# Feed-forward gate and value products with tokens on partitions instead of features, and PE transposes behind them

## The reference

```python
# block 1: a depthwise causal convolution over 3 tokens stands between the products and the gelu
h = rms_norm(x, norm_ffn_w[i])
u = causal_depthwise_conv(h @ w_ffn_up[i], w_ffn_conv[i], b_ffn_conv[i])
u_gate, u_val = jnp.split(u, 2, axis=-1)
x = x + (jax.nn.gelu(u_gate) * u_val) @ w_ffn_down[i]
# block 2
h2 = rms_norm_2(x, g_ffn[i])
x = x + (jax.nn.silu(h2 @ w_gate[i]) * (h2 @ w_up[i])) @ w_down[i]
```

## Time and profile before

| | |
|---|---|
| median of 3 runs | 2569.82 us (2569.43 to 2570.0) |
| span of the profiled execution, first to last instruction | 2567.5 us |
| median less span | 2.3 us |
| PE busy | 2548.9 us, 99% |
| DVE busy | 1534.1 us, 60% |
| ACT busy | 1082.9 us, 42% |
| mean granted TensorE clock | 0.997 |

### The profile page before, as it was taken

One profiled execution on the slowest core, in us unless ns is written; L12 is line 12 of the kernel. 1 busy time (PEld: TensorE's weight loads), 2 busy tenths in 40 slices (PEclk: granted clock), 3 DMA queues, 4 the chain that ended last, 5 costly groups with the idle time before them and its releaser, 6 DMA issues.

```text
span 2567.5 us, 37759 instructions
## 1 busy us (share of the span) xinstructions
PE 2548.9 (99%) x16088; PEld 2305.2 (90%) x16088; DVE 1534.1 (60%) x1280; ACT 1082.9 (42%) x967; POOL 41.7 (2%) x57
## 2 busy tenths in 40 slices
PE   8999999999999999999999999999999999999998
PEld 8988778999999999998888888889999999999987
DVE  4556555666666666676677656555555555555564
ACT  4344444444434444446544433343333333333353
POOL 0000000000000000000000000000000000000000
PEclk9999999999999999999999999999999999999999
DMA  7555465555555555555665555655555555555553
GB/s 263 180 155 169 147 229 185 181 180 185 191 180 188 187 180 190 185 181 184 214 201 168 181 190 186 226 180 182 190 184 181 191 184 183 192 181 186 189 188 110
DMA packets 237966, 476.77 MB, mean 186 GB/s; under 512 B 9958, under 2 KB 10534, under 8 KB 237110
## 3 DMA queue, kind: packets, MB, share of 16 engines
q1 hardware_dynamic: 234102, 459.72, 54.5%
q0 software_dynamic: 3744, 15.77, 1.8%
q10 hardware_dynamic: 32, 0.01, 0.0%
HBM read 471.28 MB, written 4.19 MB: 185 GB/s over the span
## 4 chain that ended last, share of the span: by engine, by line
PE 98%; issue 1%; DMA 0%; DVE 0%; ACT 0%; SPq 0%; POOLq 0%; POOL 0%; ACTq 0%
PE acc L1402 49%; PE acc L1395 45%; PE aux L1425 1%; DMA raw<-in_w_in 0%; PE aux L1488 0%; PE aux L1469 0%; PE aux L1567 0%; PE aux L1461 0%; PE aux L1460 0%; PE aux L1527 0%; PE aux L1552 0%; PE aux L1557 0%; ACT w_hi L595 0%; PE aux L1578 0%; PE aux L1489 0%
## 5 line engine op out<-in xcount | busy, mean ns | idle before, releaser
L1395 PE MATMUL acc<-act_hi,w_hi 128*128 128x256 f32 x3216 | 912.9, 284 | 2.5 <-DVE w_lo L822 2.5
L1395 PE MATMUL acc<-act_lo,w_hi 128*128 128x256 f32 x3216 | 911.0, 283 | 0.0
L1395 PE MATMUL acc<-act_hi,w_lo 128*128 128x256 f32 x3216 | 910.9, 283 | 0.0
L1402 PE MATMUL acc<-w_hi,act_hi 128*128 128x512 f32 x1888 | 740.8, 392 | 0.0
L1402 PE MATMUL acc<-w_hi,act_lo 128*128 128x512 f32 x1888 | 735.1, 389 | 0.0
L1402 PE MATMUL acc<-w_lo,act_hi 128*128 128x512 f32 x1888 | 735.1, 389 | 0.0
L601 ACT ACTIVATE w_hi<-raw 128x2048 fp32r<-128x2048 f32 x216 | 413.9, 1916 | 738.0 <-PE acc L1395 501.7
L822 DVE TENSOR_TENSOR w_lo<-raw,w_hi 128x2048 fp32r<-128x2048 f32 (+2 forms) x225 | 504.5, 2244 | 355.4 <-ACT w_hi L595 355.4
L595 ACT ACTIVATE w_hi<-raw 128x2048 fp32r<-128x2048 f32 (+2 forms) x225 | 422.5, 1879 | 673.3 <-PE acc L1402 490.0
L827 DVE TENSOR_TENSOR w_lo<-raw,w_hi 128x2048 fp32r<-128x2048 f32 x216 | 495.2, 2293 | 343.6 <-ACT w_hi L601 343.5
L1395 PEld LDWEIGHTS acc<-act_hi,w_hi 128*128 128x128 f32 x3216 | 616.7, 192 | 6.9 <-issue 5.7
(11 more groups left out here) (146 smaller groups left out, 737.5 us busy)
## 6 DMA issues: line engine op xcount, KB each, us to landing
raw<-in_w_in SPq DMA_DIRECT2D x104, 1024.0 KB, 5.2
raw<-in_w_ffn_up SPq DMA_DIRECT2D x88, 1024.0 KB, 5.0
raw<-in_w_ffn_down SPq DMA_DIRECT2D x44, 1024.0 KB, 5.1
raw<-in_w_gate SPq DMA_DIRECT2D x44, 1024.0 KB, 5.2
raw<-in_w_up SPq DMA_DIRECT2D x44, 1024.0 KB, 5.2
raw<-in_w_down SPq DMA_DIRECT2D x44, 1024.0 KB, 5.0
raw<-in_w_ple_gate SPq DMA_DIRECT2D x32, 1024.0 KB, 5.1
raw<-in_w_out SPq DMA_DIRECT2D x16, 1024.0 KB, 5.0
```

The source lines that it names most:

```text
L1395: mm = pe.matmul(flat[0:rows, T * f:T * f + T], w[:, c], x[:, k, :], start=start and n == 0 and f % 2 == 0, stop=stop and n == 2, skip_gro ...
L1402: mm = pe.matmul(acc[:, s, m, 0:width], x[:, k, c], w, start=start and n == 0, stop=stop and n == 2, skip_group_check=True)
```

## The change

All gate and value units use the unflipped form. Their results have tokens on partitions, so the norm factor is the per-partition scalar `r_col`, and `norm_diag` and `norm_row` are dropped for both feed-forward stages. In block 1, ACT evacuates (`up_out`) in two operations into `up_tok`; PE transposes (`up_turn`, 8 transposes) into a half of `aux`, once for the gate and once for the value of every step (22 times), and the convolution reads `aux` instead of `up_in`. In block 2, ACT evacuates the gate with the silu (`gate_silu`), DVE multiplies the value accumulator into it (`up_product`), and PE transposes the finished product (`f_turn`, once a step, 11 times); ACT and DVE split it from `aux` (`f_split`, `f_rest`). The small work moves to other slots.

```diff
+            def up_out(part, g, slot, used):          # ACT
+                act.wait_ge(unit_used, used)
+                act.wait_ge(acc_free, g)
+                act.wait_ge(r_done, 2)
+                own.order()
+                step(ACT.Copy, up_tok[part][:, 0, :], acc[:, (slot + FFN[0]["g"]) % 2, 0, :], scale=r_col[:, 0:1])
+                act.activation(up_tok[part][:, 1, :], acc[...], ACT.Copy, scale=r_col[:, 1:2]).then_inc(acc_free, 1)
+            def conv_first(it, part):                 # ACT, instead of ffn_a
+                act.wait_ge(up_turned, it * 2 + (part + 1))
+                act.wait_ge(tables_now, it + 1)
+                own.order()
+                for f in range(KU):
+                    step(ACT.Identity, (f_gate, f_val)[part][:, f, :], fours((aux01, aux23)[part])[:, f, :], conv_a,
+                         scale=conv_now[:, TAPS - 1, part, f:f + 1], bias=conv_now[:, TAPS, part, f:f + 1])
...
 # ACT, block 1: head
-                head = {3: lambda: ffn_a(b, 0, 0, g0 + 1), 5: lambda: ffn_act(b, 0, g0 + 1),
-                        7: lambda: ffn_a(b, 0, 1, g0 + 2)}
+                head = {3: lambda: up_out(0, g0, 0, u0 + 4), 4: lambda: conv_first(0, 0)}
...
+                gelu(0)
+                up_out(1, g0 + 1, 1, u0 + 8)
 # ACT, block 1: each round, after the split of slot j
+                        if j == 0:
+                            conv_first(i, 1)
+                        if j == 2:
+                            f_split(0, i)
+                        if j == 3:
+                            up_out(0, i * 6 + (g0 + 2), 0, i * 12 + (u0 + 12))
+                        if j == 4:
+                            conv_first(i + 1, 0)
...
 # DVE, block 1: each round, before the remainder of slot j
                         if j == 1:
-                            ffn_c(b, i)
+                            conv_rest(i, 1)
+                            f_product(i)
                         if j == 2:
-                            ffn_d(b, i)
+                            conv_tables(i + 1)
                         if j == 3:
-                            ffn_a(b, i + 1, 0, g0 + 2, i * 12 + (u0 + 12))
+                            f_rest(0, i)
...
 # DVE, block 1: tail
+                tail = {2: lambda: conv_tables(last), 3: lambda: f_rest(0, last - 1),
+                        5: lambda: conv_rest(last, 0), 11: lambda: f_rest(0, last, KU)}
                 for j in range(12):
...
                     if j >= 8:
-                        add_down(gt + j - 6, j - 8, ut + j + 1)
+                        add_down(gt + j - 6, gt + j - 6, j - 8, ut + j + 1)
+                    if j == 9:
+                        conv_rest(last, 1)
+                        f_product(last)
                     remainder(ut + j + SPL)
...
 # PE
+                def up_turn(step, p, g):
+                    pe.wait_ge(acc_free, g + 1)
+                    if p or not isinstance(step, int) or step:
+                        pe.wait_ge(conv_b, step * 8 + (4 if p else -4))
+                    for k in range(KU):
+                        for m in range(M):
+                            c = T * k + P * m
+                            mm = pe.transpose((aux01, aux23)[p][:, c:c + P], up_tok[p][:, m, P * k:P * k + P], ident[:])
+                    mm.then_inc(up_turned, 1)
...
-                        mm = part(f["act"], KU * q, u, g, True, q == 0, q == 3)
+                        mm = part(f["act"], KU * q, u, g, False, q == 0, q == 3)
...
 # PE, each round, after unit n
+                        if n == 0 and b == 0:
+                            up_turn(i, 1, i * 6 + (g0 + 1))
+                        if n == 4 and b == 0:
+                            up_turn(i + 1, 0, i * 6 + (g0 + 2))
+                        if n == 0 and b == 1:
+                            f_turn(i, i * 6 + (g0 + 1))
...
 # PE, head (block 1): up_turn after unit 4; tail: up_turn after units 0, 4 and 8 (block 1), f_turn after 0 and 8 (block 2)
```

More of the change, by code:

```diff
@@ L78, in __init__, with did @@
         self.eng, self.n, self.last, self.i, self.per = eng, {}, None, None, {}
-    def did(self, sem):
+    def did(self, sem, at=None):
+        if at is not None:
+            self.last = (sem, at)
+            return
         base = self.n[sem.num] = self.n.get(sem.num, 0) + 1
@@ new lines, in conv_first, with gelu @@
+            def conv_first(it, part):
[5 more added lines that the diff above has]
+                         scale=conv_now[:, TAPS - 1, part, f:f + 1], bias=conv_now[:, TAPS, part, f:f + 1])
+            def gelu(it):
+                act.wait_ge(conv_b, it * 8 + 4)
+                own.order()
+                step(ACT.Gelu_apprx_tanh, f_gate, f_gate, act_f)
@@ new lines, in gate_silu, with f_split @@
+            def gate_silu(g, slot, used):
+                act.wait_ge(unit_used, used)
+                act.wait_ge(acc_free, g)
+                act.wait_ge(r_done, 5)
+                own.order()
+                step(ACT.Silu, gate_tok[:, 0, :], acc[:, (slot + FFN[1]["g"]) % 2, 0, :], scale=r_col[:, 0:1])
+                act.activation(gate_tok[:, 1, :], acc[:, (slot + FFN[1]["g"]) % 2, 1, :], ACT.Silu, scale=r_col[:, 1:2]).then_inc(acc_free, 1)
+            def f_split(b, it, tile=0):
+                f = FFN[b]
+                if b == 0:
+                    act.wait_ge(f_full, it + 1)
@@ L707, in ffn_act @@
                 else:
-                    act.wait_ge(acc_free, freed)
+                    act.wait_ge(f_turned, it + 1)
                 own.order()
[L710 to L721, removed]
+                step(ACT.Copy, act_hi[f["f_act"]][:, tile:tile + KU, :], f_val if b == 0 else fours(aux01), f_hi)
@@ L742, in ffn @@
                         if j == 9:
-                            ffn_act(b, i + 1, i * 6 + (g0 + 3))
+                            gelu(i + 1)
                         if j == 11:
[L745 to L750, removed]
@@ L751, in ffn @@
-                for j in range(12):
-                    split(u0 + FT_TAIL + j + SPL)
+                            up_out(1, i * 6 + (g0 + 7), 1, i * 12 + (u0 + 20))
+                    own.leave(ROUNDS, (act_step, own.start[act_step.num] + 2 * ROUNDS))
+                gt, ut = g0 + G_TAIL, u0 + FT_TAIL
+                tail = {0: lambda: conv_first(last - 1, 1), 2: lambda: f_split(0, last - 1),
+                        3: lambda: up_out(0, gt, 0, ut + 4), 4: lambda: conv_first(last, 0), 6: lambda: gelu(last),
+                        7: lambda: up_out(1, gt + 1, 1, ut + 8), 8: lambda: conv_first(last, 1),
+                        10: lambda: f_split(0, last, KU)}
@@ new lines, in ffn1, with ffn2 @@
+                for j in range(12):
+                    split(ut + j + SPL)
+                    if j in tail:
+                        tail[j]()
+            def ffn2():
+                u0, g0 = FFN[1]["u"], FFN[1]["g"]
+                last = FS - 1
+                for j in range(8):
+                    split(u0 + j + SPL)
+                    for name, *args in after.get(u0 + j, ()):
+                        if name in tasks:
+                            tasks[name](*args)
+                    if j == 3:
+                        gate_silu(g0, 0, u0 + 4)
+                with act.Fori(0, ROUNDS) as i:
+                    own.enter(i, [(f_hi, 1), (act_step, 1)], (act_step, i + own.n[act_step.num]))
+                    for j in range(12):
+                        split_at(i, u0 + 8 + j + SPL)
+                        if j == 0:
+                            f_split(1, i)
+                        if j == 3:
+                            gate_silu(i * 6 + (g0 + 2), 0, i * 12 + (u0 + 12))
+                    own.leave(ROUNDS, (act_step, own.start[act_step.num] + ROUNDS))
+                gt, ut = g0 + G_TAIL, u0 + FT_TAIL
+                tail = {0: lambda: f_split(1, last - 1), 3: lambda: gate_silu(gt, 0, ut + 4),
+                        8: lambda: f_split(1, last, KU)}
+                for j in range(12):
+                    split(ut + j + SPL)
@@ L831, in did, with freed @@
                 own.did(sem)
+            def freed(g):
+                own.did(acc_free, g + 1)
             def turn(t):
@@ L1100, in gla_norm, with conv_rest @@
                         did(s)
[L1103 to L1119, removed]
+            def conv_rest(it, part):
+                dst, src = (f_gate, f_val)[part], fours((aux01, aux23)[part])
                 v.wait_ge(conv_a, it * 8 + 4 * (part + 1))
@@ L1137, in ffn_c, with up_product, f_rest @@
                 did(f_full)
-            def ffn_d(b, it, tile=0):
+            def up_product(g, slot, used):
+                v.wait_ge(unit_used, used)
+                v.wait_ge(acc_free, g)
+                own.order()
+                for m in range(M):
+                    s = acc_free if m == M - 1 else vec_step
+                    v.scalar_tensor_tensor(val_tok[:, m, :], acc[:, (slot + FFN[1]["g"]) % 2, m, :], r_col[:, m:m + 1],
```

(40 more changed lines are left out.)

146 lines of the change are left out of this document (76 added, 70 removed).

## The result

The changed kernel takes 2550.2 us in the median of 4 runs (2547.99 to 2551.14) against 2569.8 us before (2569.43 to 2570.0): 19.6 us less, a ratio of 0.9923, interval 0.9912 to 0.9935. The forecast was 2548.7. The profiled execution has a span of 2548.0 us, 19.5 less than before.

The account below looks back on a forecast made before the run. PE, busy 2548.9 of 2567.5 us, was taken as the bound. -54.8 - 0.9 + 29.7 + 2.3 + 2.2 + 0.4 = -21.1 us gives a span of 2546.4, plus 2.3 for the median: 2548.7 us, range 2543 to 2559.

Parts of the forecast that it names:

- Units: Both feed-forward stages: 176 gate and value units become unflipped, each giving back 0.3115 us, 54.8 us in all.
- Norm rows: The norm row goes twice, 0.43 us each: 0.9 us less.
- Turns: Transposes added on PE, 22 turns in block 1 and 11 in block 2, at 0.90 us each: 29.7 us more.
- rival (b): Each turn drains PE's pipe, 0.35 us more a turn, 11.6 us in all: 2560.3 us; chance 14%.
- rival (c): Transposes of freshly written data do not overlap, 0.287 us each, 75.8 us instead of 29.7: 2594.8 us; chance 4%.
- Wait in the rounds: Block 1, slot 3: PE's first down unit waits 0.26 us for `f_rest` in each of 9 rounds, 2.3 us.
- A refill of the pipe: Upper bound on the wait in block 1's rounds: 0.6 us if PE's pipe has to refill too.
- Tail: Block 1's tail: PE waits for `f_rest` before the last step's down, 2.2 us, once.
- Head: Block 1's head: the value's `up_out` stands behind the first gelu and its table load, 0.4 us, once.
- clock 1.00: Sign expected in the profile: PE's granted clock stays at 1.00, the 2.4 GHz level.
- (a): The waits for `f_done` and in block 1's tail do not appear, 4.9 us less: 2543.8 us; chance 12%.
- (d): Gate and value are bound by something other than form, so the 54.8 falls away: 2603.5 us; 2% with the page's matmul rule.

Follow-up runs that it names:

- e6_halves: On e3_all, gate and value matmuls each move 256 columns instead of 512, so 48 a unit, weights still moving: 2597.32 us.
- e4_twice: On the changed kernel, each of the 33 new turns makes its 8 transposes twice: 2579.14 us.
- e1_rounds: On the changed kernel, in block 1's rounds `f_split` goes from slot 2 to 1 and `f_rest` from slot 3 to 2: 2545.83 us.
- e3_all: On the changed kernel, the reorderings of e1_rounds and e2_tail, and in block 1's head the value's `up_out` ahead of the first gelu: 2542.69 us.
- e7_best_again: The same kernel as e3_all, run again on another occasion: 2542.12 us.
- e2_tail: On the changed kernel, block 1's tail only: last step's taps and product before slot 9's add, `f_split` in slot 9, `f_rest` in 10: 2546.47 us.

## Why the prediction was right, and where it was off

Against its own span the forecast was 21.1 us less, and it came to 19.5. By its steps:

- Units, 54.8 us given back: right. The expectation of e6_halves was this term alone, and 55.2 came out; the 256- and 512-wide starts in the trace, 0.120 and 0.227, were the same in the new units. The Trainium skill's step of columns over 2.4 GHz plus about 2.5 ns ("TensorE: Matmul & The Clock Gate", section "Wait — 56ns, not 53.3ns?") is refuted for these fp32r matmuls twice, by the total and by e6_halves.
- Norm rows, 0.9: no such matmuls are left in these stages; as taken.
- Turns, 29.7: measured 28.9 (33 x 0.875), and about as much again when doubled. The lower end of the bounds held; the drained pipe, rival (b), and the 0.287 us a transpose, rival (c), are both out by e4_twice. So is the reading of the Trainium skill's 275 ns ("TensorE: Matmul & The Clock Gate", section "Part 4: PE-mode transpose") as a price: it is the size of one transpose's duration in the trace (a median of 273 ns for the new ones), not of its step. What that section says of such transposes and the clock no run here tests: the granted clock was 1.00 in a turn of 16 and in the 22 us behind it (e4_twice).
- Wait in the rounds, 2.3: the wait itself was right to 0.01 us, but the restart after it costs some 0.1 us more. A round took 67.49 or 67.45 where e1_rounds has 67.07 to 67.1: 0.4 each, 3.4 in all. A refill of the pipe had stood among the bounds, not in the sum.
- Tail, 2.2: measured 2.04. Head, 0.4: measured 0.62, because ACT needed 0.11 us between gelu and `up_out`, whose two operations then took 0.59 and 0.68, and PE followed 0.13 later.
- Not in the sum at all: 1.7 us of low clock behind the tail's wait. The prediction took waits at their length and said "clock 1.00" for the whole; this is the step that failed, in size a tenth of the effect.

Summed with what was measured: -54.8 - 0.9 + 28.9 + 3.4 + 2.0 + 0.6 + 1.7 = -19.1, against -19.5 in the span. Block 1's part of this is -27.4 - 0.4 + 19.3 + 3.4 + 2.0 + 0.6 + 1.7 = -0.8, as its chain has it; the 0.4 that remain are block 2's, where a unit took (66.20 - 0.875) / 12 = 5.444 us instead of 5.447, over 130 units. That the error of the total was no larger is in part luck: the low clock and the restarts, 2.8 us, were missing, and the turns were taken 0.8 too dear.

Of the rivals, (a), no waits, is what e3_all makes true by another order: it gives 2542.7, 1.1 under that rival's figure, 0.8 of it because a turn costs 0.875 and not 0.90; the low clock and the restarts were in neither figure. (d) is out by the step of 0.227 us in the new units and by e6_halves.

## What to carry to other kernels

Where PE is busy all the time, take the step from start to start and not the duration of a matmul: here, halving the number of matmuls for the same columns gave back some 13 ns for each one dropped. The 96 dropped over the four units of a group are worth 1.25 us, and the eight transposes that the new layout needs cost 0.87, so it pays, and pays most where two groups share a turn, as in block 2. After a change that moves small work between slots, walk through every wait of the busy engine with the start times of the other engines: one operation placed behind instead of ahead of a 2.3 us subtraction cost 0.4 us a round. A wait of PE was dearer than its length, by about 0.1 us of restart in the rounds, and behind the tail's 2 us by 1.7 us more, nearly all of it low clock.

## What the runs showed of the hardware that was not expected

A pause of TensorE of about 2 us, behind a long stretch without one, was followed by 3.4 to 3.5 us at half clock in all three profiled executions that have it: from the first matmul on in the changed kernel, some 1 us later in e1_rounds and e4_twice. The granted clock over the first 4 us was 0.57, 0.62 and 0.66. The waits of 0.3 to 0.6 us left it at 1.00.

A second place of low clock lies at the start of the program, which the change does not touch, and it explains differences that belong to no edit. Among the first 192 matmuls, which start near 18 us, PE steps by 0.21 us instead of 0.12 up to a moment that differs from one execution to the next: 20.8 us in e7_best_again, 22.9 in e3_all, 23.8 in e1_rounds. The same kernel on two occasions, e3_all and e7_best_again, in the chain:

```profile
17.82 25.48 PE acc L1477 x192
```

```profile
17.88 24.56 PE acc L1477 x192
```

At the end of this piece the two are 0.86 us apart, and their spans, 2540.5 and 2539.7, differ by 0.8. Over all nine profiles the piece takes 24.56 to 25.94 us. Two groups of runs about 1 us apart are also found in the kernel before (2569.0 to 2569.4 and 2569.9 to 2570.3 us beside e1_rounds), so this is the likely source of the pairs of e2_tail, whose profiled run is of the longer pair and has 25.88 us here. The three kernels with the tail's wait spread by 2.7 to 3.2 us, more than the 1.4 us that this place gives, and the others by 0.2 to 1.7; an execution that sometimes escapes the low clock behind the wait would fit, but none has been traced. The mean clock of a run does not settle it: the profiled execution of e4_twice has slow matmuls in both places and a mean of 0.998, since its granted clock stands at 1.00 where its first matmuls step by 0.21 us. Where the two differ, go by the steps.
